# Rounded half and remainder of the activations side by side in one matmul, in the 256-token feed-forwards and dense experts

## The reference, cut to what matters

```
def swiglu(h, w1, w3, w2):
    return (jax.nn.silu(h @ w1) * (h @ w3)) @ w2

# moe_swiglu: out = out + gates[..., e:e+1] * swiglu(h, w1[e], w3[e], w2[e]) for 8 experts
```

## Time and profile before

| | |
|---|---|
| median of 3 runs | 2849.24 us (2844.79 to 2849.41) |
| profiled execution, span from first to last instruction | 2846.7 us |
| PE busy | 2721.4 us (96%), 17542 matmuls |
| PEld busy | 2445.6 us (86%) |
| DVE busy | 1914.3 us (67%) |
| ACT busy | 1182.8 us (42%) |
| POOL busy | 118.6 us (4%) |
| mean granted TensorE clock | 0.989 |
| HBM read | 508.24 MB, 179 GB/s over the span |

### The profile page before, as it was taken

How to read it: one execution, slowest core, us unless ns; L and a number is a source line. 1 busy time by engine, 2 the same in 40 slices (tenths; PEclk the granted TensorE clock), 3 DMA queues, 4 the chain that set the end, 5 groups by cost and what they waited for, 6 DMA issues and landing times.

```text
span 2846.7 us, 43022 instructions
## 1 busy us (share of the span) xinstructions
PE 2721.4 (96%) x17542; PEld 2445.6 (86%) x17542; DVE 1914.3 (67%) x2703; ACT 1182.8 (42%) x1510; POOL 118.6 (4%) x227
## 2 busy tenths in 40 slices
PE   3979999999999998899999999999999999999999
PEld 3879998899999998888888988888888888886999
DVE  5877778765877787877577545764666646676655
ACT  3435445453443576742132423422225213265543
POOL 0010000000000000000000000000000000000000
PEclk9989999999999999999999999999999999999999
DMA  7676766645666697845455223453544535311554
GB/s 295 222 248 228 266 223 210 226 137 171 230 237 218 232 342 264 276 135 188 147 174 173 88 90 104 152 169 111 166 156 130 165 123 163 121 60 46 175 185 145
DMA packets 116619, 511.97 MB, mean 180 GB/s; under 512 B 12608, under 2 KB 16064, under 8 KB 116304
## 3 DMA queue, kind: packets, MB, share of 16 engines
q1 hardware_dynamic: 81776, 381.92, 39.8%
q0 software_dynamic: 32112, 117.45, 12.6%
q10 hardware_dynamic: 2544, 9.96, 0.9%
HBM read 508.24 MB, written 1.05 MB: 179 GB/s over the span
## 4 chain that ended last, share of the span: by engine, by line
PE 77%; DVE 12%; ACT 4%; issue 3%; DMA 3%; ACTq 0%; DVEq 0%; POOLq 0%
PE PS L2095 22%; PE PS L2096 22%; PE PS L2097 22%; DVE wlo L1098 5%; ACT whi L571 2%; DVE ada L1130 1%; PE PS L2289 1%; DMA ada_first<-in_adastream 1%; PE PS L2286 1%; PE PS L2285 1%; DMA ada<-in_adastream 1%; PE PS L2190 1%; PE PS L2191 1%; PE PS L2194 1%; DVE PS L1130 1%
## 5 line engine op out<-in xcount | busy, mean ns | idle before, releaser
L571 ACT ACTIVATE whi<-raw 128x1408 fp32r<-128x1408 f32 (+2 forms) x540 | 718.3, 1342 | 789.8 <-PE PS L2097 731.6
L1098 DVE TENSOR_TENSOR wlo<-raw,whi 128x1408 fp32r<-128x1408 f32 (+2 forms) x540 | 840.2, 1577 | 223.8 <-ACT whi L571 222.9
L2095 PE MATMUL PS<-h_hi,whi 128*128 128x256 f32 (+1 forms) x2656 | 861.9, 325 | 15.2 <-DVE wlo L1098 8.2
L2096 PE MATMUL PS<-h_lo,whi 128*128 128x256 f32 (+1 forms) x2656 | 858.4, 323 | 0.0
L2097 PE MATMUL PS<-h_hi,wlo 128*128 128x256 f32 (+1 forms) x2656 | 857.3, 323 | 0.0
L2095 PEld LDWEIGHTS PS<-h_hi,whi 128*128 128x128 f32 x2656 | 499.9, 188 | 62.8 <-DVE wlo L1098 11.4
L2097 PEld LDWEIGHTS PS<-h_hi,wlo 128*128 128x128 f32 x2656 | 500.0, 188 | 42.2
L2096 PEld LDWEIGHTS PS<-h_lo,whi 128*128 128x128 f32 x2656 | 499.9, 188 | 41.5 <-issue 0.2
L2095 PE MATMUL PS<-hid_hi,whi 128*128 128x256 f32 (+1 forms) x1298 | 416.0, 320 | 4.3 <-DVE wlo L1098 4.3
L2096 PE MATMUL PS<-hid_lo,whi 128*128 128x256 f32 (+1 forms) x1298 | 414.2, 319 | 0.0
L2097 PE MATMUL PS<-hid_hi,wlo 128*128 128x256 f32 (+1 forms) x1298 | 414.2, 319 | 0.0
(11 more groups left out here) (464 smaller groups left out, 3243.4 us busy)
## 6 DMA issues: line engine op xcount, KB each, us to landing
raw<-in_wstream SPq DMA_DIRECT2D x243, 704.0 KB, 4.5
raw<-in_wstream SPq DMA_DIRECT2D x176, 768.0 KB, 5.5
ada<-in_adastream POOLq DMA_DIRECT2D x222, 512.0 KB, 4.5
raw<-in_wstream SPq DMA_DIRECT2D x121, 512.0 KB, 4.0
ada_first<-in_adastream ACTq DMA_DIRECT2D x6, 1536.0 KB, 22.5
X<-in_xT SPq DMA_DIRECT2D x1, 1024.0 KB, 13.4
X<-in_ctxT SPq DMA_DIRECT2D x1, 1024.0 KB, 5.6
cond<-in_c_rows POOLq DMA_DIRECT2D x1, 1024.0 KB, 5.8
```

Of the source, the lines that this page charges most:

```text
L571: nc.scalar.activation(whi[:, (q + dp) % SLOTS, 0:n], raw[:, (q + dp) % RAW_SLOTS, 0:n], ACT.Copy).then_inc(hi_split, 1)
L1098: nc.vector.tensor_tensor(wlo[:, (q + dp) % SLOTS, 0:n], raw[:, (q + dp) % RAW_SLOTS, 0:n], whi[:, (q + dp) % SLOTS, 0:n].bitcast(F32), AL ...
L2095: mm(o, left[0], right[0], start=start, stop=False)
L2096: mm(o, left[0], right[1], start=False, stop=False)
```

## The change

In the units of the dense feed-forward, of the dense experts and of the last feed-forward (all with 256 moving columns) `h_hi` and `h_lo` become two parts of one tile `h_pair`. The tile hi-weights x (h_hi beside h_lo) is one matmul of 512 columns into a whole bank, and lo-weights x h_hi one of 256 columns into the bank's first half: two matmuls (`beside`) in place of three. The sum of a bank's two halves is made afterwards: ScalarE copies the second halves of both banks of a unit into `stage_a` (`unit_copy`), VectorE adds the first halves to it (`unit_sum`), ScalarE takes the SiLU in SBUF, VectorE multiplies. Rounding and low half of a unit (`hid_high`, `hid_low`, `dense_high`, `dense_low`) are moved behind the copy and the sum of the next one, except in the last unit. In the experts TensorE now waits for the sum of group n - 2 where it waited for the product. Kept as before: units 0 and 1 of the dense and of the last feed-forward's first half, the first two units of expert 0, all second projections, the 512-token feed-forwards.

```diff
@@ build: tiles
-            h_hi[SEQ] = sb("h_hi1", [PART, KD, SEQ], F32R, s)
-            h_lo[SEQ] = sb("h_lo1", [PART, KD, SEQ], F32R, s)
+            h_pair = sb("h_pair", [PART, 2, KD, SEQ], F32R, s)
+            h_hi[SEQ], h_lo[SEQ] = h_pair[:, 0], h_pair[:, 1]
...
+        def in_columns(T, i, u):
+
+            return T == SEQ and (i > 0 or u >= 2)
@@ ScalarE, ffn
+            def unit_copy(u, bank):
+
+                nc.scalar.activation(stage_a[:, u % 2, :].rearrange("p (b t) -> p b t", b=2), PS[:, bank:bank + 2, SEQ:BOTH],
+                                     ACT.Copy).then_inc(unit_copied, 1)
...
+                        if in_columns(T, i, u):
+                            unit_copy(u, 2 * (u % 3))
+                            if u and in_columns(T, i, u - 1):
+                                hid_high(u - 1, i)
+                            act.wait_ge(unit_summed, SUMMED0[name, i] + u + 1)
+                            src = stage_a[:, u % 2, 0:T]
+                        else:
+                            src = PS[:, 2 * (u % 3), 0:T]
+                        nc.scalar.activation(stage_a[:, u % 2, 0:T], src, ACT.Silu).then_inc(silu_done, 1)
+                        if u == UNITS - 1 or not in_columns(T, i, u):
+                            hid_high(u, i)
@@ VectorE, ffn
+            def unit_sum(u, bank):
+
+                dve.wait_ge(unit_copied, summed[0] + 1)
+                summed[0] += 1
+                x = stage_a[:, u % 2, :].rearrange("p (b t) -> p b t", b=2)
+                nc.vector.tensor_tensor(x, x, PS[:, bank:bank + 2, 0:SEQ], ALU.add).then_inc(unit_summed, 1)
...
+                        if in_columns(T, i, u):
+                            unit_sum(u, 2 * (u % 3))
+                            if u and in_columns(T, i, u - 1):
+                                hid_low(u - 1, i)
+                            gate_out = stage_a[:, u % 2, T:2 * T]
+                        else:
+                            gate_out = PS[:, 2 * (u % 3) + 1, 0:T]
                         dve.wait_ge(silu_done, UNITS * (e0 + i) + u + 1)
+                        nc.vector.tensor_tensor(stage_b[:, u % 2, 0:T], stage_a[:, u % 2, 0:T], gate_out, ALU.mult).then_inc(evacuated, 1)
+                        if u == UNITS - 1 or not in_columns(T, i, u):
+                            hid_low(u, i)
@@ TensorE
+            def beside(bank, left, pair, start, stop):
+
+                mm(PS[:, bank, :].rearrange("p (s t) -> p s t", s=2), left[0], pair, start=start, stop=False)
+                return mm(PS[:, bank, 0:SEQ], left[1], pair[:, 0, :], start=False, stop=stop)
...
+                        if T == SEQ and tile < up:
+                            ins = beside(2 * (group % 3) + bank, weights(p0 + panel, at), h_pair[:, :, k, :], k == 0, k == depth - 1)
+                        else:
+                            ins = passes(PS[:, 2 * (group % 3) + bank, 0:T], weights(p0 + panel, at),
+                                         (act_in[0][:, k, 0:T], act_in[1][:, k, 0:T]), k == 0, k == depth - 1)
@@ TensorE, dense experts
-                        pe.wait_ge(S("moe_out"), n - 1)
+                        r2, g2 = divmod(n - 2, UNITS + 4)
+                        if g2 < UNITS and in_columns(SEQ, r2, g2):
+                            pe.wait_ge(unit_summed, SUMMED0["moe", r2] + g2 + 1)
+                        else:
+                            pe.wait_ge(S("moe_out"), n - 1)
```

More of the change, by code:

```diff
@@ L456, in build @@
         ORDER = [n for n, _, _ in PHASES]
+        SUMMED0, _n = {}, 0
+        for _name in ("dense", "moe", "ffn11"):
+            for _i in range(DENSE if _name == "moe" else 2):
+                SUMMED0[_name, _i] = _n - (2 if _i == 0 else 0)
+                _n += UNITS - (2 if _i == 0 else 0)
+        def in_columns(T, i, u):
+            return T == SEQ and (i > 0 or u >= 2)
         def runs(name):
@@ L673, in ffn, with hid_high @@
                 full = PANEL * PART
+                def hid_high(u, i):
+                    act.wait_ge(evacuated, g0 + u + 1 + EXPERT_GROUPS * i)
+                    nc.scalar.activation(hid_hi[T][:, u, :], stage_b[:, u % 2, 0:T], ACT.Copy).then_inc(hid_hi_done, 1)
                 for i in range(n):
@@ L2284, in ffn @@
                                 pe.wait_ge(evacuated, g0 - 1 + EXPERT_GROUPS * i)
-                            mm(bank, left[0], right[0], start=k == 0, stop=False)
-                            mm(bank, left[1], right[0], start=False, stop=False)
+                            if not columns:
+                                mm(bank, left[0], right[0], start=k == 0, stop=False)
+                                mm(bank, left[1], right[0], start=False, stop=False)
                         h_chunk(norm_of_h, k, half)
                         for o, (bank, left, right) in enumerate(tiles):
-                            ins = mm(bank, left[0], right[1], start=False, stop=k == KD - 1)
+                            if columns:
+                                ins = beside(o, left, h_pair[:, :, k, :], k == 0, k == KD - 1)
+                            else:
+                                ins = mm(bank, left[0], right[1], start=False, stop=k == KD - 1)
                             if places[o][1] == PANEL - 1:
@@ L2664, in moe @@
                                 need(tile)
-                                ins = passes(PS[:, 2 * (n % 2) + b, 0:SEQ], weight(tile), half(h if g < UNITS else hid, k), k == 0, k == depth - 1)
+                                if g < UNITS:
+                                    ins = beside(2 * (n % 2) + b, weight(tile), h_pair[:, :, k, :], k == 0, k == depth - 1)
+                                else:
+                                    ins = passes(PS[:, 2 * (n % 2) + b, 0:SEQ], weight(tile), half(hid, k), k == 0, k == depth - 1)
                                 mark(ins, tile, b and k == depth - 1)
```

54 lines of the change are left out of this document (35 added, 19 removed).

## The result

The changed kernel takes 2860.35 us (median of 4 runs, 2858.61 to 2862.27), the kernel before, run beside it, 2847.01 (4 runs, 2843.32 to 2849.41): a ratio of 1.0045, 95% interval 1.0031 to 1.0058. The change makes the kernel slower by 0.45%, about 13 us, where 2855.5 was forecast with a range of 2847 to 2863. The profiled execution took 2858.61 us, with a span of 2856.9 (before: 2846.7). As a change, +6.3 us was forecast; it is +13.3 by the medians and +10.2 by these two spans.

The account below looks back on a forecast made before the run. TensorE (77% of the chain) was taken to bound the kernel, VectorE (12%) second. +8.2 - 2.2 - 4.3 + 4.6 = +6.3 us on a 2846.7 span gave 2853.0, with 2.5 added 2855.5; range 2847 to 2863.

Parts of the forecast that it names:

- the late low half: Second projections of dense and last feed-forward: TensorE waits 1.15 us for an operand at k = 10, four times, +4.6 us.
- rival A: Whole kernel: VectorE's chain and the late unit eat the gain, +6.3 us, own spread +2 to +11; chance 0.45.
- rival E: Wide matmul's moving operand in two runs costs 6.8 ns, so 976 tiles gain nothing: +6.5, in all +13 us; chance 0.08.
- VectorE's unit: Chain per unit grows from 1.24 to 1.49 us; experts' steps from 6.01 to 6.26; experts 1 to 3 lose 8.2 us.
- the last unit's 1.15: Last unit of an expert or half, where nothing is pipelined: sum to split takes 2.39 us, +1.15.
- The tile: TensorE, changed units: one wide plus one narrow matmul take 346.6 ns instead of 353.3, 6.7 saved.
- the 4.3 us of the feed-forwards: Dense and last feed-forward, where VectorE has room: 640 tiles save 6.7 ns each, -4.3 us.
- The 2.2 us in the experts: The 21 of 42 expert units paced by TensorE: 336 tiles save 6.7 ns each, -2.2 us.
- B: Slack cushions the last unit's +1.17 in three experts (-3.5) and half of the four waits (-2.3): +0.5 us; chance 0.17.
- C: Narrow matmul runs at the load's pitch, 12.5 ns saved in 976 TensorE-paced tiles: +0.6 us; chance 0.12.
- D: Lengthened waits in three experts drop the granted clock to half speed, +6 us, in all +12; chance 0.10.
- F: VectorE's added work is hidden everywhere and all 1312 tiles gain: -8.8 us, 2840; chance 0.08.

Follow-up runs that it names:

- Experiment 4: Changed kernel with the dense experts put back to three matmuls a tile and the old unit chain: 2852.17 us, 1.0015 of the kernel before.
- experiment 6: Changed kernel with the modulation tiles of experts 2 and 3 spread over groups 1, 3, 5, 7, 9, 11, 12, 13: 2853.13 us, ratio 1.0012.
- experiment 3: Changed kernel with the copy, SiLU and rounding of each feed-forward half's last unit ahead of the two panels ScalarE rounded first: 2855.45 us, 1.0032.
- 1: Changed kernel with rounded half and remainder stored adjacently, so the wide matmul's moving operand is one run of 512 columns: 2858.38 us, 1.0039.
- 2: Changed kernel with the operand's two halves stored adjacently but the access pattern still written as two runs of 256: 2862.52 us, one run.
- 7: Kernel before the change, with only the modulation tiles of experts 2 and 3 spread out: 2845.38 us, ratio 0.9984.
- experiment 12: Same kernel as experiment 9, profiled once more on another chip: 2837.98 us in one run, the kernel before beside it 2849.21.
- experiment 5: Changed kernel with eight wide matmuls, then eight narrow ones per output tile in both feed-forwards, units 2 to 10 of each half: 2857.98 us, 1.0034.
- experiment 9: Changed kernel with grouped widths and early last-unit copy in the feed-forwards, three passes and spread modulation tiles in the experts: 2840.47 us, 0.9977.

## Why the prediction was right, and where it was not

**The sign and the places were right, the size was not.** VectorE's chain and the late low half outweigh what TensorE gains. 2860.35 lies in the range, 4.9 above the forecast, but just beyond rival A's own spread (up to 2860.2): the range holds it because it took in rival E. And the forecast stood on 2849.24 for the kernel before, which is 2847.01 over four runs. As a change, +13.3 us is twice the +6.3 of the forecast. Point by point:

- **VectorE's unit: right.** 1.52 us from sum to split for 1.49, steps of 6.28 for 6.26. From the gating of one expert's group 11 to that of the next, experts 1, 2 and 3 are 2.4, 3.1 and 2.2 us longer, 7.7 in all for 8.2. Within expert 2 the sum of +3.0 is right and its parts fall elsewhere: 1.05 us come before product 2, where the added sum first delays it (43.13 us from the last expert's gating before, 44.18 after), 2.2 over the eight steps, and nothing behind product 10, where I had put the last unit's 1.15. There the stretch from product to split (two links of the chain, unchanged) is as long as before. Experiment 4 shows the whole term by taking it away, experiment 6 shows its condition: the modulation tile in the same unit.
- **The late low half: right.** 1.02 us in the timeline for 1.15, 4.66 us in all for 4.6 (experiment 3).
- **The tile: this step failed.** "New tile: 228.8 + 117.8 = 346.6 ns, 6.7 saved" adds two pitches, each read where a matmul follows its like. No row of the kernel before has a wide matmul behind a narrow one, and I put no bound on that change: I bounded only the operand in two runs. In turns, the pair takes 353.3 ns, or 348.9. So the 4.3 us of the feed-forwards did not come, and that is the whole error there: +5.1 us measured for +0.3.
- **The 2.2 us in the experts did not come either; that the stage hit its forecast (+6.2 for +6.0) is luck.** Expert 0 was 1.4 us shorter after the change (66.64 us from its first product to its first gating, 68.08 before), but not by the joined tile. In nine of the fourteen profiles of this study the granted clock is 0.50 for a moment near 600 us, and in these nine, joined or not, expert 0 takes 67.9 to 68.2 us; in the five others (after, 1, 2, 7, 12) it takes 66.5 to 66.7. Experiment 3, whose experts are those of the kernel after, has that stretch, and its experts take 397.77 us, 7.9 more than before. With 7.7 for the chain, 4.7 for the waits and nothing for the tile the change adds up to 12.4 us, against 13.3 by the medians. The stretch in experiment 3 (columns of the earlier trace rows):

```profile
602.00:604.00 2.00, 2.00 (x7) 1.72 (x8) 1.90 (x5) 0.00 (x0) 0.00 (x0) 0.50 0.61 128
```

- **Rival E** had the size (no saving in the tile, +13 us; 13 measured) and the wrong reason: experiments 1 and 2 clear the operand's two runs, experiment 5 convicts the order. An unknown was priced right by a bound meant for another one.
- **Rivals B, C, D and F are out.** The waits are not cushioned (B). The tile is not 12.5 ns shorter (C); 8.6 ns on average is the most seen, and only in groups of eight. The granted clock stays at 1.00 through the stages, even in 600 to 608, where it was 0.50 for a moment before (D); the drop that D feared comes in kernels of both kinds, costs some 1.4 us, and here it fell on the kernel before. VectorE's unit stays above TensorE's 5.65 us in the experts (F); but experiment 6 shows how near F was: spreading the modulation tiles brings the units to 5.64.
- **The Trainium skill**, "TensorE: Matmul & The Clock Gate", section "Back-to-back issue gap": by its N / 2.4 + 2.5 ns the wide matmul would follow after 215.8 ns and the pair take 2.5 ns less than three; measured are 230.0 or 234.0 and no saving against the 353.3 in turns, 228.6 or 229.3 and a saving of 8.6 ns in groups. The page's figures for like matmuls in a row say nothing on changing N from one matmul to the next, and here that decides.

**What stays open.** Why turns cost some 7 to 9 ns a tile is not known; the runs show only that neither the operand's layout nor its description does it, and that weights taken in turns do not do it to narrow matmuls. The grouped order was tried in the feed-forwards alone, not in the experts, where the pair still takes turns. What sets the pace (last section) is open too. It moves a stage of one profile by some us, and the medians over 9 to 11 runs average over it.

## What to carry to other kernels

A pitch read where a matmul follows its like holds only there: before matmuls of different widths are merged or mixed, bound the cost of the change of width, and prefer runs of equal widths within an accumulation. Merging saves only the fixed part of one instruction (here 7 ns), so each operation that it adds must fall where its engine has time of its own, and the last unit of a stage has none. An engine near its limit is best relieved by spreading its side work: one line that moved modulation tiles gave the kernel before 0.16% and 0.12% in two measurements.

## What the runs showed of the hardware

**Order of widths.** The same eight wide and eight narrow matmuls take 8 x 353.3 = 2.83 us in turns and 2.76 in groups: 234.0 ns behind a wide one and 119.3 behind a narrow one in turns, 229 and 116 on average in groups.

**Two paces at full clock.** With a granted clock of 1.00, TensorE runs 256-column matmuls either 117.8 or 113.3 ns apart (340.0 ns for three), the pair in turns at 353.3 or 348.9. Stretches of one pace last from a few us to over 180 (the whole dense feed-forward of the kernel before). Two changes in that kernel, at 656.8 and 863.4 us, came with a start of TensorE that was 0.7 or 0.8 us late; in the grouped order the narrow blocks change between 118.0 and 113.4 from one to the next without any pause. In the kernel before nearly all of the dense experts' units ran at the slower pace. In experiments 9 and 12, one program, the faster pace fell on expert 2 once and on expert 3 once: first product to gating of group 11 took 847.11 - 785.65 = 61.46 us at 340.0 ns a tile in experiment 9, and 845.46 - 781.57 = 63.89 at 353.3 in experiment 12. That is 2.4 us an expert, where the runs of one kernel here spread over 4 to 14 us, and a reason to take the effect of an edit from medians and the pace of a tile from its own starts, not from one span.

**The clock's cost.** A granted clock of 0.50 for a moment near 600 us makes expert 0 1.4 us longer, in whichever kernel it falls. Two profiles whose clocks differ there can't be compared over that stage before this is taken off.
